# Seven small changes of order and of waits in a two-layer hybrid transformer step

## The reference, cut to what matters

```
z  = rmsnorm(x) @ w_in                 # 768 c_q, 256 c_kv, 32 k_r, 512 x_r, 512 g_r
q  = rmsnorm(c_q) @ w_uq               # 8 heads x (64 + 32 rotary)
kv = rmsnorm(c_kv) @ w_ukv             # 8 heads x (64 key + 64 value)
y  = RG-LRU(conv(x_r)) * gelu(g_r)     # the recurrent group, 512 wide
o  = softmax(q k^T, chunk-causal) v    # the attention group, 512 wide
h  = x + concat(rmsnorm(o), rmsnorm(y)) @ w_out
x' = h + square(relu(rmsnorm(h) @ w_up)) @ w_down      # 1024 -> 4096 -> 1024
```

## Time and profile before

| | us |
|---|---|
| median of 3 runs (2753.32 to 2754.3) | 2753.4 |
| the profiled execution | 2753.91 |
| its span, from the first to the last instruction | 2752.0 |
| PE busy in it | 2662.0 (97%) |
| DVE busy | 1323.3 (48%) |
| ACT busy | 807.6 (29%) |
| POOL busy | 341.2 (12%) |
| share of PE in the chain that ended last | 89% |

### The profile page before, as it was taken

One profiled execution on the slowest core, in us unless ns is written; L12 is line 12 of the kernel. 1 busy time (PEld: TensorE's weight loads), 2 busy tenths in 40 slices (PEclk: granted clock), 3 DMA queues, 4 the chain that ended last, 5 costly groups with the idle time before them and its releaser, 6 DMA issues.

```text
span 2752.0 us, 36936 instructions
## 1 busy us (share of the span) xinstructions
PE 2662.0 (97%) x15742; PEld 2566.6 (93%) x15742; DVE 1323.3 (48%) x1435; ACT 807.6 (29%) x1240; POOL 341.2 (12%) x216
## 2 busy tenths in 40 slices
PE   8999999899999999999999999998999999999996
PEld 8999877799999999999999997778999999999995
DVE  7898766564223223223379986655632222321223
ACT  4344355332112112022224425552320120210221
POOL 0123343120000000000201404421100000000001
PEclk9999999999999999999999999999999999999998
DMA  3111101211111111111211120021111111111111
GB/s 139 54 62 58 55 10 42 79 47 47 46 45 40 47 46 46 44 42 62 95 62 57 47 87 18 18 81 47 46 46 46 39 47 47 46 46 39 46 46 64
DMA packets 43401, 143.44 MB, mean 52 GB/s; under 512 B 8256, under 2 KB 9376, under 8 KB 43248
## 3 DMA queue, kind: packets, MB, share of 16 engines
q1 hardware_dynamic: 36896, 124.19, 13.3%
q0 software_dynamic: 4768, 11.45, 1.4%
q10 hardware_dynamic: 1584, 5.54, 0.5%
HBM read 127.37 MB, written 11.44 MB: 50 GB/s over the span
## 4 chain that ended last, share of the span: by engine, by line
PE 89%; DVE 6%; DMA 2%; issue 1%; ACT 1%; POOL 0%; SPq 0%; DVEq 0%; ACTq 0%; POOLq 0%
PE ps L792 55%; PE ps L563 21%; PE ps L728 4%; PE ps L743 4%; PE ps L675 2%; PE ps L700 1%; PE ps L609 1%; DVE wlo L1184 1%; DMA qo<-mt 1%; PE ps L579 1%; DVE xall L1599 1%; DVE t L1188 0%; DVE rs L1188 0%; DVE osqt L1194 0%; DMA comp<-sum_scratch 0%
## 5 line engine op out<-in xcount | busy, mean ns | idle before, releaser
L1609 DVE TENSOR_TENSOR wlo<-raw,whi 128x1024 fp32r<-128x1024 f32 x126 | 154.4, 1225 | 921.2 <-ACT whi L1119 921.1
L1119 ACT ACTIVATE whi<-raw 128x1024 fp32r<-128x1024 f32 x126 | 133.6, 1060 | 984.2 <-PE ps L792 984.1
L792 PE MATMUL ps<-xmh,whi 128*128 128x358 f32 x1536 | 337.0, 328 | 5.8 <-issue 5.8
L792 PE MATMUL ps<-xml,whi 128*128 128x358 f32 x1536 | 338.0, 328 | 0.0
L792 PE MATMUL ps<-fl,whi 128*128 128x358 f32 x1536 | 337.3, 327 | 0.0
L792 PE MATMUL ps<-fh,wlo 128*128 128x358 f32 x1536 | 336.5, 327 | 0.0
L792 PE MATMUL ps<-xmh,wlo 128*128 128x358 f32 x1536 | 336.4, 327 | 0.0
L792 PE MATMUL ps<-fh,whi 128*128 128x358 f32 x1536 | 336.2, 327 | 0.0
L792 PEld LDWEIGHTS ps<-xmh,whi 128*128 128x128 f32 x1536 | 265.4, 190 | 6.3 <-issue 6.3
L792 PEld LDWEIGHTS ps<-fh,wlo 128*128 128x128 f32 x1536 | 266.8, 189 | 0.0
L792 PEld LDWEIGHTS ps<-xmh,wlo 128*128 128x128 f32 x1536 | 266.7, 189 | 0.0
(11 more groups left out here) (277 smaller groups left out, 3922.0 us busy)
## 6 DMA issues: line engine op xcount, KB each, us to landing
raw<-in_wst SPq DMA_DIRECT2D x204, 512.0 KB, 3.4
xall<-in_xT SPq DMA_DIRECT2D x11, 537.0 KB, 7.4
x_scratch<-xall POOLq DMA_DIRECT2D x8, 537.0 KB, 3.6
out_yT<-xall SPq DMA_DIRECT2D x8, 537.0 KB, 3.6
rc<-sum_scratch POOLq DMA_DIRECT2D x16, 268.0 KB, 4.0
xall<-in_xT ACTq DMA_DIRECT2D x5, 537.0 KB, 6.0
xall<-x_scratch ACTq DMA_DIRECT2D x5, 537.0 KB, 6.3
ra<-qr SPq DMA_DIRECT2D x16, 134.2 KB, 2.4
```

Source lines behind the costliest of these rows:

```text
L792: mm = nc.tensor.matmul(ps[:, 3 * slot_of(u) + q, 0:CH], wt, (rh if c == "h" else rl)[kk](q), start=(kk == 0 and i == 0), stop=(kk == 7 an ...
L1119: nc.scalar.activation(whi[b % 2][:, :], raw[b % 2][:, :], ACT.Copy).then_inc(S["w_hi"], 1)
L1609: V.tensor_tensor(wlo[b % 2][:, :], raw[b % 2][:, :], whi[b % 2][:, :].bitcast(F32), ALU.subtract).then_inc(S["w_lo"], 1)
```

## The change

Eleven edits in five stretches of a layer; each is done in both layers, except where head 0 is named, which is the first head of a layer.

1. Queries. ACT makes cqh 4 and 5 before it divides block 22. DVE scales CQ5 before the low halves of CQ2 and CQ3, and multiplies y by its 1/rms behind split(26) and not ahead of split(24).
2. Head 0. The transposition of its maxima (PE) and `shift_hi` (ACT) stand after value tile 5 and not 6. `kslot_lo(1)` of DVE stands behind the reductions at tile 4 and not at tile 0; the first row sum waits for it, as it is written over the rows that kslot_lo reads.
3. Odd heads. POOL stores the inverses where it did, but copies them to the partitions only behind `few_shifts`.
4. First output products. PE waits for the last head's o_ev, s_ev, mxt and mt_lo before the second product and not before the first. DVE does `divide(3)` behind two `add_y` and split(31), and `add_y(2)` ahead of `o_low(3)`.
5. Residual loop. split(36) to split(39) stand with the odd elements 1, 3, 5 and 7 and not ahead of the even ones and behind the loop: on ACT ahead of the element's wait for res_add, on DVE between its sum and its low half. PE's first two MLP products wait for the scaled value to have been taken from the slot (oo_ev 7 and 8), and not for the sum (res_add 7 and 8).

```diff
 PE:
-                    if t == 6:
+                    if t == 5:
                         max_rows(0)
...
-                w("o_ev", 3 * NH)
-                w("s_ev", 3 * NH)
-                w("mxt", NH)
-                w("mt_lo", NH)
                 for bi, ms in enumerate(OY_TILES):
                     for n, m in enumerate(ms):
                         i = OY_ORDER.index(m)
+                        if i == 1:
+                            w("o_ev", 3 * NH)
+                            w("s_ev", 3 * NH)
+                            w("mxt", NH)
+                            w("mt_lo", NH)
                         product(to_slot(U_OY[i]), U_OY[i], B_OY + bi, 512 * n, [tok(t) for t in yh], [tok(t) for t in yl],
...
-                        if k < 2:
+                        if k < 2 and first:
+                            w("oo_ev", 7 + k)
+                        elif k < 2:
                             pe.wait_ge(S["res_add"], L * PER["res_add"] + gg * 8 + (7 + k))
 ACT:
                 cq_high(2)
                 cq_high(3)
-                split(22)
                 cq_high(4)
                 cq_high(5)
+                split(22)
                 cq_square(5)
...
-                    if t == 6:
+                    if t == 5:
                         shift_hi(0)
...
                 for m in range(8):
-                    if m and m % 2 == 0:
-                        split(35 + m // 2)
+                    if m % 2 == 1:
+                        split(36 + m // 2)
                     w("res_add", m + 1)
...
-                split(B_MLP + 1)
 DVE:
                 split(21)
+                scaled(U_CQ[5], cq[5], rs, "cq_ev")
                 cq_low(2)
                 cq_low(3)
-                scaled(U_CQ[5], cq[5], rs, "cq_ev")
                 cq_low(4)
                 cq_low(5)
...
                 rstd(t3, SUM_Y)
-                for c in range(4):
-                    V.tensor_tensor(g[c][:, :], g[c][:, :], t3[:, :], ALU.mult).then_inc(S["y_n"], 1)
                 split(24)
...
                 scaled(U_UQ[3], qn[1], rs, "qn")
                 split(26)
+                for c in range(4):
+                    V.tensor_tensor(g[c][:, :], g[c][:, :], t3[:, :], ALU.mult).then_inc(S["y_n"], 1)
                 turn(1)
...
+                    if h == 0 and n == 0:
+                        w("kslot_lo", 2)
                     r = slice(64 * (h % 2), 64 * (h % 2) + 1)
...
                             if h == 0:
                                 kslot_hi(1)
-                                kslot_lo(1)
...
                                 reduce_max(h + 1, MX_AT.index(i))
+                            if h == 0 and i == 4:
+                                kslot_lo(1)
...
                     o_low(j)
-                divide(3)
                 add_y(0)
                 add_y(1)
                 split(31)
+                divide(3)
+                add_y(2)
                 o_low(3)
-                add_y(2)
                 split(32)
...
                 for m in range(8):
-                    if m and m % 2 == 0:
-                        split(35 + m // 2)
                     if m == 0:
                         w("oy_ev", 8)
                         w("o_sum", 3)
                     scaled(U_OO + m, osqt, rs, "oo_ev")
                     w("oo_ev", m + 1)
                     V.tensor_tensor(x[m], x[m], osqt[:, :], ALU.add).then_inc(S["res_add"], 1)
+                    if m % 2 == 1:
+                        split(36 + m // 2)
                     w("xm_hi", m + 1)
                     lo(xml[m][:, :], x[m], xmh[m][:, :], "xm_lo", col(V_MG + m))
-                split(B_MLP + 1)
 POOL:
-                def spread_inverse(j):
+                def store_inverse(j):
 
                     w("inv", j + 1)
                     pool.dma_start(flat_sums(j), comp[:, :]).then_inc(S["inv_out"], 16)
+
+                def copy_inverse(j):
+
                     w("inv_out", 16 * (j + 1))
                     for e in range(2):
                         pool.dma_start(rc[half(e), 0:TOK], sum_scr[2 * j + e:2 * j + e + 1, :].to_broadcast([64, TOK])).then_inc(S["inv_in"], 16)
...
                     low_parts(h)
                     if h % 2 == 1 and h >= 3:
-                        spread_inverse((h - 3) // 2)
+                        store_inverse((h - 3) // 2)
                     few_shifts(h)
-                spread_inverse(3)
+                    if h % 2 == 1 and h >= 3:
+                        copy_inverse((h - 3) // 2)
+                store_inverse(3)
+                copy_inverse(3)
```

## The result

The changed kernel takes 2718.9 us (median of 4 runs, 2717.99 to 2719.8) against 2753.36 before (4 runs, 2752.59 to 2754.3): ratio 0.9875, 95% interval 0.9858 to 0.9892. The profiled execution has a span of 2717.5 us.

What follows compares the result with a forecast made beforehand. PE's waits, in five places per layer, were taken to bound the kernel. Gains 6.2 + 3.2 + 7.6 + 2.5 + 9.2 = 28.7 us off 2753.9 gave 2725.2, stated as 2725.0; range 2719 to 2732.

Steps and rivals of the forecast that it cites:

- the queries' term: Query products: earlier CQ5 scaling and high halves and later y scaling gain 3.1 us a layer, 6.2 in all; bounds 4.1, 6.7.
- 0.3 to 0.5 of wait at split(22): Second query product: split(22), held as before by POOL's addition, still leaves PE this wait; gain there 1.0 us.
- Head 0: First head of each layer: earlier transposition and later kslot_lo gain 3.2 us in all; bounds a loss of 2.8 and 4.4.
- the gain ascribed to the transposition: Head 0: transposing the maxima one tile earlier brings only 0.4 us, 0.9 in layer 2, because of the rotary copy.
- Odd heads: Heads 3, 5 and 7: inverse copies behind the shift rows gain 7.6 us of 8.1 waited; bounds 5 and 8.1.
- The residue of 0.5: Odd heads: wait expected to remain, PE standing 0 to 0.4 us a head; subtracted from 8.1.
- First output products: After the last head: the first residual sum comes 1.2 us earlier a layer, 2.5 in all; bounds 2 and 4.
- Residual loop: Residual loop and first MLP products: PE becomes the bound, wait and slow start go, 9.2 us; bounds 5.8 and 9.5.
- DVE staying the bound: Second rival, residual loop: POOL's additions hold DVE more than counted, 9.2 shrinks to 1.3 a layer; 2731.5 us, chance 0.10.
- the late queue behind split(22): Third rival, queries: split(27) late beyond its 1.1 us cover eats the y edit; 2727 to 2729; queries or head 0 short 0.11.
- SP's wait for y: Slower case: late y delays rotary rows and head 0's first score tile; 2754 us and up; chance of slower 0.01.
- the first rival: Odd heads: shift rows stay late, SP's rows colliding with POOL's copies across queues; most of 8.1 stays, 2731 us, chance 0.12.

Runs made afterwards that it cites:

- e9: Changed kernel with 56 added waits, odd MLP products also waiting for the next weight block's high half: 2798.87 us, 1.0167 of before.
- e1: Kernel before with the three query edits alone: 2744.09 us, 0.9959 of before.
- e5: Changed kernel with DVE's first two residual sums and POOL's first addition of squares moved further ahead: 2695.26 us, 0.9788 of before.
- e8: Kernel before with kslot_lo behind the third group of reductions alone: 2752.12 us, 0.9993 of before.
- e12: Kernel before with head 0's transposition one value tile earlier alone: 2753.65 us, 0.9999 of before.
- e3: Kernel before with POOL's edit alone, inverse copies behind the shift rows: 2744.55 us, 0.9963 of before.
- e6: Kernel before with the edits of the first output products alone: 2750.96 us, 0.9992 of before.
- e10: Kernel before with the residual loop's four weight splits moved alone, PE's condition kept: 2743.81 us, 0.9962 of before.
- e11: Kernel before with PE's first MLP products waiting for oo_ev instead of res_add alone, splits kept: 2747.72 us, 0.9978 of before.
- e2: Kernel before with head 0's edits alone, transposition one tile earlier and kslot_lo later: 2749.16 us, 0.9988 of before.

## Why the prediction was right or wrong

The mechanisms were right nearly everywhere and the sum was too small. The step that failed is the queries' term: 6.2 forecast, 9.9 measured, 3.7 of the 5.8 missing. It was mis-sized in three ways, worth 1.6, 1.5 and 0.5.

- It priced three waits at what the list gives (0.43, 0.90, 2.04). A wait costs PE more. The list counts from the modelled end of the last matmul (0.33 long), while matmuls start 0.165 apart; and the first group behind a wait starts its successor 0.6 later instead of 0.5. In PE's timeline before, groups of three start 0.49 apart, up to the wait:

```profile
239.56 0.65 PE L563 MATMUL ps<-cqh,wlo 128*128 128x358 f32 x3
240.64 0.77 PE L563 MATMUL ps<-cqh,whi 128*128 128x358 f32 x3 [0.43 <-DVE cql L1201]
241.25 0.66 PE L563 MATMUL ps<-cql,whi 128*128 128x358 f32 x3
```

  From 239.56 to 241.25 is 1.69 where two steps take 0.99: 0.70 lost, 0.43 listed. This 0.27, three times in each of two layers, is 1.6. e9 measured 0.23 on 54 waits.
- It left out the slow stretch behind the 2.04 in layer 2, 1.5. The granted clock there was 0.90 of full speed, against 1.00 at the same place of layer 1; the engine had stood for 2.04 just before in both:

```profile
275.70:293.00 17.30, 17.30 (x105) 17.30 (x106) 14.60 (x13) 2.05 (x2) 0.00 (x0) 1.00 0.47 132
1629.40:1646.00 16.60, 16.53 (x91) 16.53 (x92) 14.65 (x14) 2.05 (x2) 0.00 (x0) 0.90 0.46 125
```

  (Columns: stretch, us, busy us of PE, PEld, DVE, ACT and POOL, granted clock, DMA share, GB/s.) I had seen 26.66 against 25.14 for the same 144 matmuls and not priced it. Such a place was slow in 6 of the 18 that the nine traces with this wait have, so it is worth 0.5 on average and 1.5 when it falls.
- It kept 0.3 to 0.5 of wait at split(22), assuming that POOL's addition would again be first. DVE came first by 0.02 and POOL was held instead (2.88), so the split took 0.95 and not the 2.86 of before:

```profile
239.30 0.95 DVE L1186 TENSOR_TENSOR wlo<-raw,whi 128x768 fp32r<-128x768 f32 x1
```

```profile
239.32 2.88 POOL L1684 TENSOR_TENSOR sqa<-sqa,sqa 128x1074 f32<-128x1074 f32 x1 [7.88 <-ACT sqa L937]
```

  By the rule of the Trainium skill (SBUF — State Buffer, Who interferes with whom) whichever begins first holds the other; the trace agrees. Which of them begins first followed from the forecast's own numbers: POOL had led by 0.2 (241.65 against 241.86), DVE's queue moved forward by 1.3 and POOL's addition by 1.0, so DVE would lead by 0.1. DVE led by 0.02 to 0.04 in both layers of every trace with these edits (the changed kernel, e1, e5, e9).

Point by point for the rest:

- Head 0: 3.2 forecast, 2.6 measured. That kslot_lo would be held only by POOL's second subtraction, and that a short wait would come at the sixth score tile, was right (0.51 and 0.52, forecast 0.7). Wrong was the gain ascribed to the transposition, 0.4 and 0.9: the sixth score tile is timed by DVE's copies, which wait for the last value tile. e8 and e12 show it. The 0.4 between the end of DVE's rotary copy and the first score tile (326.41 to 326.84) was read as slack and was none. With the transposition earlier PE waits for that copy, and the tile again starts 0.47 behind the copy's end, 25.44 after the key product where it was 25.46 (in layer 2 25.48 where it was 25.90, and that 0.4 was lost again by the sixth tile):

```profile
320.05 0.83 DVE L1464 CAST koh<-kpe 64x1296 fp32r<-64x1296 f32 x1
```

```profile
321.35 0.48 PE L675 MATMUL ps<-koh,qo 128*128 128x144 f32 x3 [1.03 <-DVE koh L1464]
...
327.93 0.51 PE L675 MATMUL ps<-koh,qo 128*128 128x144 f32 x2 [0.51 <-DVE mxp L1474]
```

- Odd heads: 7.6 forecast, 9.0 measured, above the upper bound of 8.1. The cause was right (e3: POOL's order). The residue of 0.5 didn't appear, and the time gained exceeds the 8.1 listed by 0.9, some 0.15 a wait. That is less than the 0.23 to 0.27 of the products; what a wait costs among score tiles was not measured by itself.
- First output products: 2.5 and 2.8. The part that the edit sets was 1.2 a layer, as forecast: the sum begins at 498.11, where the low half before it ends at 494.88 + 3.19 = 498.07. The remainder is the round trip through memory (5.44 and 5.42 us for comp<-sum_scratch before, 4.77 and 5.84 after), which varies. That the first product's earlier start brings nothing was right: without the transfers 1.2 a layer is all that e6 and the changed kernel gained.
- Residual loop: 9.2 and 8.9. Right in mechanism and size; e10 adds that the splits alone do it.
- The 1.3 before the queries is no part of the change. That it went the same way as the error is chance.
- The rivals: DVE staying the bound, the late queue behind split(22) and SP's wait for y are all absent from PE's list after. Of the first rival the time failed and the mechanism held: in the kernel before, the copies did delay SP's rows from another queue, and the waits went because the rows now move before the copies' packets do.

The range was drawn from upper bounds that all lacked the cost beyond the list. Those bounds (6.7, 4.4, 8.1, 4 and 9.5) add up to 32.7, which is 2720.7 on the scale of the median; the range went down to 2719, lower than its own reason, and the measured 2718.9 lies 1.8 below what the bounds give.

## What to carry to other kernels

Price a removed wait of a matmul stream by the distance of starts across it, not by the listed idle: here each was worth 0.23 to 0.27 us more in the products and some 0.15 among score tiles, and about 1.5 more where the clock fell behind it. Where two edits aim at one wait, ask which chain times the next tile: the transposition and PE's new condition brought nothing, because another chain or another edit already did. Before taking the distance between a releaser's end and its follower's start for slack, look at what the same pair shows where it is known to wait. And look for an instruction that PE needs and that stands in a queue behind a wait it has no part in: moving two sums and an addition ahead was worth 23.6 us, two thirds of what all eleven edits gave together.

## What the runs showed of the hardware

- How long PE stood did not by itself decide whether its granted clock fell to the lower level. In the dense products no wait of 1.2 to 1.6 us was followed by it (54 in e9, two in e11), waits of 2.04 were in 6 of 18 places, at a cost of 1.5 us, and those of 2.9 before the MLP in all 16, at a cost of 1.5 to 3.0 over the next 72 matmuls. Behind the waits of about 10 us 108 matmuls took 19.3 to 20.7, against 17.8 at full pace. Among the score tiles the order is not kept: behind a wait of 1.6 in e8 and one of 1.7 in e3 the clock was low, behind one of 2.9 in e11 and one of 3.0 in e2 it was not. In the rows, in that order, the granted clock is the third number from the end:

```profile
1782.90:1787.00 4.10, 4.07 (x15) 3.09 (x16) 0.00 (x0) 1.02 (x6) 4.04 (x2) 0.58 0.00 0
330.00:335.00 5.00, 4.88 (x18) 3.61 (x19) 3.20 (x9) 1.29 (x5) 4.13 (x2) 0.66 0.00 0
389.00:397.00 8.00, 7.61 (x44) 6.18 (x44) 4.58 (x14) 3.67 (x17) 6.73 (x3) 1.00 0.00 1
387.00:395.00 8.00, 7.93 (x45) 6.36 (x45) 4.89 (x14) 3.96 (x18) 6.28 (x3) 1.00 0.00 1
```

- A small transfer issued by POOL behind two large ones of its own queue took 4.5 us; issued just ahead of them, 2.4 at most in that window. SP's small transfers, in another queue, were held by the same two large ones: their packets moved 2.3 to 4.4 us after the issue behind them, 1.2 to 2.1 after it ahead of them.
- Where DVE and POOL held each other off, the order turned on a few hundredths of a microsecond: at split(22) POOL ahead of DVE by 0.2 cost DVE 1.9 us (2.86 for 0.95), DVE ahead by 0.02 cost it nothing.
